# One product of 128 columns for the index key, the gates and the index weights, instead of two

## The reference, cut to what matters

```python
h = rms_norm(x, norm_mix[l])
(m_qk, m_v, m_o, m_i, m_f, r_x, r_g, a_q, a_k, a_v, a_qi, a_ki, a_w, gates) = jnp.split(
    h @ w_in[l], split_at, axis=-1)
...
qi = apply_rope(a_qi.reshape(B, S, IDX_HEADS, IDX_DIM), cos, sin)
ki = apply_rope(a_ki[:, :, None, :], cos, sin)[:, :, 0, :]
...
# in the attention, per block of queries:
logits = jnp.einsum('bqhd,bsd->bqhs', qib.astype(f32), k_idx_f) * (IDX_DIM ** -0.5)
score = jnp.einsum('bqh,bqhs->bqs', wb.astype(f32) * (IDX_HEADS ** -0.5), jax.nn.relu(logits))
```

## Time and profile before

| | us |
|---|---|
| runs, median of 3 (lowest, highest) | 3902.78 (3896.48, 3905.8) |
| profiled execution, device time | 3901.3 |
| profiled execution, span of the core | 3899.5 |
| PE busy | 3705.6 (95%) |
| DVE busy | 2175.3 (56%) |
| ACT busy | 1370.8 (35%) |
| mean granted TensorE clock | 0.972 |

### The profile page before, as it was taken

One profiled execution on the slowest core, in us unless ns is written; L12 is line 12 of the kernel. 1 busy time (PEld: TensorE's weight loads), 2 busy tenths in 40 slices (PEclk: granted clock), 3 DMA queues, 4 the chain that ended last, 5 costly groups with the idle time before them and its releaser, 6 DMA issues. The chain is left out here.

```text
span 3899.5 us, 57931 instructions
## 1 busy us (share of the span) xinstructions
PE 3705.6 (95%) x24033; PEld 3058.4 (78%) x24033; DVE 2175.3 (56%) x2934; ACT 1370.8 (35%) x1537; POOL 0.2 (0%) x4
## 2 busy tenths in 40 slices
PE   7998889999999988899999999899999999899998
PEld 6787778888877877788888777887888778888887
DVE  6896345766358963457663656554232566553233
ACT  5553332443255533324422333033222342033223
POOL 0000000000000000000000000000000000000000
PEclk9999999999999999999999999999999999999999
DMA  3321122554222211225542231022222331032332
GB/s 109 88 73 55 54 68 95 178 199 151 87 82 85 69 55 55 69 94 178 199 149 88 88 126 49 3 105 81 97 97 89 96 119 35 14 118 77 97 97 75
DMA packets 272985, 364.68 MB, mean 94 GB/s; under 512 B 22428, under 2 KB 218640, under 8 KB 271504
## 3 DMA queue, kind: packets, MB, share of 16 engines
q1 hardware_dynamic: 247824, 311.45, 25.0%
q10 hardware_dynamic: 24960, 50.33, 3.7%
HBM read 351.79 MB, written 9.96 MB: 93 GB/s over the span
## 5 line engine op out<-in xcount | busy, mean ns | idle before, releaser
L248 PE MATMUL banks<-act_hi,w_hi 128*128 128x512 f32 x4208 | 1686.7, 401 | 31.8 <-issue 9.9
L250 PE MATMUL banks<-act_hi,w_lo 128*128 128x512 f32 x4208 | 1658.2, 394 | 0.0
L249 PE MATMUL banks<-act_lo,w_hi 128*128 128x512 f32 x4208 | 1657.5, 394 | 0.0
L170 DVE TENSOR_TENSOR w_lo<-w_raw,w_hi 128x2048 fp32r<-128x2048 f32 (+1 forms) x280 | 629.5, 2249 | 746.6 <-ACT w_hi L164 744.9
L248 PEld LDWEIGHTS banks<-act_hi,w_hi 128*128 128x128 f32 x4208 | 803.3, 191 | 238.7 <-issue 59.1
L250 PEld LDWEIGHTS banks<-act_hi,w_lo 128*128 128x128 f32 x4208 | 800.7, 190 | 173.0
L249 PEld LDWEIGHTS banks<-act_lo,w_hi 128*128 128x128 f32 x4208 | 802.7, 191 | 167.2 <-issue 4.3
L164 ACT ACTIVATE w_hi<-w_raw 128x2048 fp32r<-128x2048 f32 (+1 forms) x280 | 526.8, 1882 | 933.7 <-PE banks L250 892.3
L2057 DVE SCALAR_TENSOR_TENSOR arena<-arena,small 128x512 f32<-128x512 f32 (+1 forms) x168 | 126.3, 752 | 15.6 <-issue 4.3
L248 PE MATMUL banks<-w_hi,act_hi 128*128 128x256 f32 x384 | 111.7, 291 | 3.2 <-DVE w_lo L170 3.2
L249 PE MATMUL banks<-w_lo,act_hi 128*128 128x256 f32 x384 | 110.0, 286 | 0.0
(11 more groups left out here) (363 smaller groups left out, 3602.3 us busy)
## 6 DMA issues: line engine op xcount, KB each, us to landing
w_raw<-in_w_in SPq DMA_DIRECT2D x98, 1024.0 KB, 5.4
w_raw<-in_ffn_up SPq DMA_DIRECT2D x48, 1024.0 KB, 5.3
arena<-in_ada_w ACTq DMA_DIRECT2D x24, 2048.0 KB, 8.1
w_raw<-in_w_gu SPq DMA_DIRECT2D x44, 1024.0 KB, 5.0
w_raw<-in_ffn_down SPq DMA_DIRECT2D x24, 1024.0 KB, 4.9
w_raw<-in_w_down SPq DMA_DIRECT2D x20, 1024.0 KB, 5.1
w_raw<-in_w_out SPq DMA_DIRECT2D x16, 1024.0 KB, 4.9
w_raw<-in_w_branch SPq DMA_DIRECT2D x12, 1024.0 KB, 5.0
```

The lines of the kernel that those rows point to most:

```text
L170: self.core.nc.vector.tensor_tensor(view(self.lo[:, s]), view(self.raw[:, s]), view(self.hi[:, s]).bitcast(FP32), ALU.subtract)\
L248: nc.tensor.matmul(out, wh, ah, start=first, stop=False)
L249: nc.tensor.matmul(out, wh, al, start=False, stop=False)
L250: return nc.tensor.matmul(out, wl, ah, start=False, stop=last)
```

## The change

Slot 0 of misc now holds 64 key columns once, 4 gate columns, 28 columns from the index weights on (8 are used) and 32 from the other gate on (4 are used): one product of 24 matmuls, all in bank 1. Slot 1 of misc is loaded with 8 columns that nothing uses, and PE signs it off without a product. The key is rotated on 64 partitions (`key_dve`), and a DVE copy puts it on the other 64.

With this the order changes. ACT rounds aqi's slot 1 first and its slot 0 behind the copies from bank 1; DVE does the rest of slot 1, the key, the forget gate, and then the rest of slot 0. PE still takes aqi's tiles in the order 0, 1, 2, 3. The core of the diff (line numbers after `+` are those of the changed kernel):

```diff
@@ -962,15 +962,16 @@
         def misc(i, s):
-            if s == 0:
-                return [(raw[0][:, :, 0:64], win[:, :, C_AKI:C_AKI + 64]),
-                        (raw[0][:, :, 64:128], win[:, :, C_AKI:C_AKI + 64])]
-
-            return [(raw[1][:, :, 0:32], win[:, :, C_MIF:C_MIF + 32]),
-                    (raw[1][:, :, 32:64], win[:, :, C_MIF + 4:C_MIF + 36]),
-                    (raw[1][:, :, 64:128], win[:, :, C_AW:C_AW + 64])]
+            if s:
+                return [(raw[1][:, :, 0:8], win[:, :, C_MIF:C_MIF + 8])]
+
+            return [(raw[0][:, :, 0:64], win[:, :, C_AKI:C_AKI + 64]),
+                    (raw[0][:, :, 64:68], win[:, :, C_MIF:C_MIF + 4]),
+                    (raw[0][:, :, 68:96], win[:, :, C_AW:C_AW + 28]),
+                    (raw[0][:, :, 96:128], win[:, :, C_MIF + 4:C_MIF + 36])]
 
         part = lambda b: b.rearrange("p (k n) -> p k n", k=8)[:, :, 0:128]
+        unused = lambda b: b.rearrange("p (k n) -> p k n", k=8)[:, :, 0:8]
...
-            Section("misc", 1, misc, view=(part, part), dmas=(2, 3)),
+            Section("misc", 1, misc, view=(part, unused), dmas=(4, 1)),
...
-        aw_rows = A[64:72, self.RX + 3, :]
+        aw_rows = A[64:76, self.RX + 3, :]
...
         def misc_pe(pe):
             um = u["misc"]
+            pe.wait_ge(ring.split[1], um + 1)
+            pe.sem_inc(ring.tile[1], 1)
+            pe.sem_inc(ring.done[1], 1)
             pe.wait_ge(ring.split[0], um + 1)
-            pe.wait_ge(ring.split[1], um + 1)
-            for s in (0, 1):
-                if um:
-                    pe.wait_ge(ring.bank_free[2 * s + 1], um)
-                for k in range(KD):
-                    if s == 0:
-                        pe.wait_ge(n.lo, k + 1)
-                    wh, wl = (b[:, s].rearrange("p (k n) -> p k n", k=8)[:, k, 0:128] for b in (ring.hi, ring.lo))
-                    last = three_pass(nc, ps[:, 2 * s + 1, :], (wh, wl), (self.hi[:, k, :], self.lo[:, k, :]),
-                                      k == 0, k == KD - 1)
-                last.then_inc(ring.done[s], 1)
+            if um:
+                pe.wait_ge(ring.bank_free[1], um)
+            for k in range(KD):
+                pe.wait_ge(n.lo, k + 1)
+                wh, wl = (b[:, 0].rearrange("p (k n) -> p k n", k=8)[:, k, 0:128] for b in (ring.hi, ring.lo))
+                last = three_pass(nc, ps[:, 1, :], (wh, wl), (self.hi[:, k, :], self.lo[:, k, :]), k == 0, k == KD - 1)
+            last.then_inc(ring.done[0], 1)
             pe.sem_inc(ring.tile[0], 1)
-            pe.sem_inc(ring.tile[1], 1)
...
@@ -1345,18 +1344,17 @@
         def act_part(act):
             um = u["misc"]
-            self.schedule.hi(act, um + 1, 0)
-            self.wait_tile(act, um, 1)
-            for q in range(4):
+            self.schedule.hi(act, um + 1, 1)
+            act.wait_ge(ring.done[0], um + 1)
+            for q in (0, 1):
                 ins = nc.scalar.activation(turned[1][32 * q:32 * q + 32, :],
                                            ps[32 * swapped(q):32 * swapped(q) + 32, 1, :], ACT.Copy)
             ins.then_inc(turn_ok, 1)
-            act.wait_ge(ring.done[1], um + 1)
-            nc.scalar.activation(R0, ps[32:36, 3, :], ACT.Copy)
-            nc.scalar.activation(R1, ps[0:4, 3, :], ACT.Copy)
-            nc.scalar.activation(aw_rows, ps[64:72, 3, :], ACT.Copy)
+            nc.scalar.activation(R0, ps[96:100, 1, :], ACT.Copy)
+            nc.scalar.activation(R1, ps[64:68, 1, :], ACT.Copy)
+            nc.scalar.activation(aw_rows, ps[64:76, 1, :], ACT.Copy)
             act.drain().then_inc(rows_ok, 1)
-            self.schedule.hi(act, um + 1, 1)
+            self.schedule.hi(act, um + 1, 0)
...
+        def key_dve(dve):
+
+            low = slice(0, 64)
+            key = A[:, self.KI, :]
+            dve.wait_ge(turn_ok, 1)
+            tt_(key[low], ps[low, 1, :], cos[low], ALU.mult)
+            tt_(turned[1][low], turned[1][low], sin[low], ALU.mult)
+            dve.drain()
+            tt_(key[low], key[low], turned[1][low], ALU.add)
+            dve.drain()
+            nc.vector.tensor_copy(key[64:128], key[low]).then_inc(turn_used, 1)
+
         def forget_dve(dve):
             dve.wait_ge(rows_ok, 1)
+            dve.sem_inc(ring.bank_free[1], 1)
             dve.wait_ge(bias_in, 32)
-            dve.sem_inc(ring.bank_free[3], 1)
...
@@ -1632,12 +1643,12 @@
             if after is None:
                 dve.wait_ge(table_in, 16)
+            for b in (0, 2, 3):
+                dve.sem_inc(ring.bank_free[b], 1)
+            self.schedule.lo(dve, um + 1, 1)
+            key_dve(dve)
+            forget_dve(dve)
             self.schedule.lo(dve, um + 1, 0)
-            rope_dve(dve, 1, A[:, self.KI, :], 1)
-            dve.sem_inc(ring.bank_free[0], 1)
-            dve.sem_inc(ring.bank_free[2], 1)
-            forget_dve(dve)
-            self.schedule.lo(dve, um + 1, 1)
             lambda_dve(dve)
```

More of the change, by code:

```diff
@@ L1141, in aw_pe @@
             for tt in range(ST):
-                last = nc.tensor.transpose(ps[:, 6, 8 * tt:8 * tt + 8], aw_rows[:, tt * P:tt * P + P],
-                                           self.c("ident")[64:72, 64:72])
+                last = nc.tensor.transpose(ps[:, 6, 16 * tt:16 * tt + 12], aw_rows[:, tt * P:tt * P + P],
+                                           self.c("ident")[64:76, 64:76])
             last.then_inc(aw_t, 1)
@@ L1486, in index_weights_dve @@
             dve.wait_ge(aw_t, 1)
-            ts_(gate_tm[:, :, 8:16], ps[:, 6, 0:32].rearrange("p (t c) -> p t c", t=ST), A_HEADS ** -0.5, None, ALU.mult)
+            ts_(gate_tm[:, :, 8:16], ps[:, 6, 0:64].rearrange("p (t c) -> p t c", t=ST)[:, :, 4:12], A_HEADS ** -0.5, None,
+                ALU.mult)
             dve.drain()
```

## The result

Slower, as forecast, and by about what was forecast. In nine runs of each kernel the changed kernel took 3910.18 us in the median (3907.27 to 3912.35) and the kernel before 3896.88 (3896.0 to 3905.8): ratio 1.003, 95% interval [1.002, 1.004], which is 8 to 16 us. The medians lie 13.3 us apart. The forecast was +10.4 us on top of the three runs' 3902.8, rounded to 3912, and slower with a chance of 0.66. The profiled execution took 3912.35 us, its span 3910.6, which is 11.1 more than that of before.

A forecast was written before the change was run, and what follows sets the result against it. PE, busy 95%, and what it waits for were taken to bound the kernel. Two later starts of aqi (3.64 each) and slow clocks (2.0 each), less 0.85, gave +10.4 us on 3902.8: 3912, range 3904 to 3920.

The forecast's parts named there:

- The product was cover: Under the removed misc product, 5.46 us a layer, ACT and DVE did the slot 0 work that aqi needs to start.
- The start of aqi: PE's time between the starts around aqi goes from 6.19 to 9.83 us, +3.64 a layer, waiting for DVE's slot 0 rest.
- the stretch from the rest of slot 1 to the key: On DVE ahead of aqi: 2.42 us from the start of slot 1's rest to the start of the key.
- The copy: DVE's key copy across partitions ahead of aqi: 0.45 us with its gap, bounds 0.42 and 0.69.
- The clock: PE's slow clock in aqi's first tile, behind the 9.8 us idle stretch, costs 2.0 us a layer, bounds 1.3 to 2.6.
- The lower bound: Slow clock's low bound: 2.66 us at granted clock 0.50 behind a 5.24 us wait, times 0.47, 1.3 us a layer.
- The norm: Norm ahead of misc in layer two: narrower slot 1 rounding brings the root earlier, -0.85 us; nothing in layer one.
- Given back: Behind aqi's first tile: DVE idles 2.25 us there, so neither backlog nor credit is carried on, counted as nothing.
- The second rival: Early DVE work removes PE's later waits for DVE's rest, 2.3 us in two places: +5.8 us, 3908; chance 0.07.
- Sum: Whole kernel: 2 x 3.64 + 2 x 2.0 - 0.85 = +10.4 us, forecast 3912 us.

The follow-up runs named there:

- e3_slot0_first: The changed kernel with slot 0 rounded ahead of all copies on ACT and its rest ahead of the key on DVE: 3900.68 us against 3901.78 before.
- e1_slots: The changed kernel with misc's two slots exchanged, so the one product reads slot 1: 3894.04 us against 3901.78 for the kernel before.
- e4_filler: The changed kernel with 40 unread matmuls behind the product of misc in each layer: 3908.64 us, ratio 1.0019 to the kernel before.
- before_again: The kernel before, unchanged, run once more for a second profile: 3903.14 us against 3901.3 in the first.
- e5_early_round: e1_slots with misc's wide slot rounded ahead of the norm's last square in layer two: 3894.3 us against 3901.73 for the kernel before.
- e2_forget_last: The changed kernel with DVE's rest of slot 0 moved ahead of the forget gate's four operations: 3909.89 us, ratio 1.0026 to the kernel before.

## Why the prediction was right

**The product was cover.** As forecast, its removal left the chain rounding, rest and start bare; e3_slot0_first shows it, since slot 0 comes ahead of the copies and the key there and the start still gains only 1.4 of 5.46 us; e1_slots shows that a free slot makes more of the saving real, 3.6 us.

**The start of aqi.** Forecast +3.64 a layer, measured +3.28 and +3.26. The term that was too large is the stretch from the rest of slot 1 to the key: the prediction took 2.42 us from the earlier trace rows, where DVE was itself waiting for ACT's four copies, which ended at 50.75 + 2.40 = 53.15; with the turned key there in time it is 2.21. The rest is ACT, whose rounding starts 0.54 behind the last activation's start and not 0.66, overlapping its end. The copy was taken at 0.45 and measured 0.45 to the next operation; three operations on 64 partitions take what they took on 128. DVE and not ACT came last, by 1.8 us (forecast 2.0).

**The clock.** Forecast 2.0 a layer, measured 1.7 and 2.9 with e4_filler as the comparison. Layer two lies above the bounds from the rows, 1.3 to 2.6. The lower bound was read loosely: of the 9 matmuls in those 2.66 us of the earlier trace rows four were transposes of 128 columns and five had 512, not "about 6". The Trainium skill (TensorE: Matmul & The Clock Gate, Part 1) says that the number of slow matmuls of one kernel varies, 6, 11 or 14 (it doesn't give their width; the prediction took 512 columns), and the prediction's estimate from it reached up to 2.9. The traces agree on the spread, with 9 and 14 behind waits of the same 9.3 us, but here it lay between the layers: the second execution had 9 and 14 again.

**The norm.** Forecast -0.85, measured 1.19 - 0.34 = 0.85. In layer one nothing, as forecast: DVE's wait for PE's transposed parameters grew from 3.23 to 4.22 us instead. The last activation does start 0.8 us earlier there than in the first trace of before (45.54, 46.34), but so it does in before_again (45.36), so this isn't the change's.

**Given back.** Forecast nothing, and in sum it was nothing: PE's later waits for DVE's rest are 0.4 us shorter in layer one and 0.35 longer in layer two. The second rival named this place and took 2.3 us a layer there.

**Sum.** Forecast +10.4, the traces' sum is 4.66 + 6.47 - 0.85 = +10.3. That the terms' errors cancel (0.7 too much at the start, 0.6 too little for the clock) is luck. So is it that 3912 came so near to 3910: it was counted from 3902.8, the median of three runs of before, and with nine runs that median is 3896.88 and the step 13.3.

## What to carry to other kernels

Before a product is taken out, ask what ran under it: on an engine that is 95% busy its length is not the gain, but only what the next chain leaves of it: here 1.4 of 5.5 us with slot 0 first, 3.6 with the slots exchanged, and less than nothing in the order of the change. In a ring of slots, sign off first the slot that the next consumer reads first, and put the long-lived product into the other. A VectorE operation on 4 rows took as long as one on 128 here (0.47 and 0.42 us over 512 elements), so look where it stands: four of them in front of what PE waited for cost 1.8 us.

## What the runs showed of the hardware

- The same wait of 9.3 us was followed by 9 slow matmuls in one layer and 14 in the other, and by the same two numbers in a second execution. Of the four waits of 2.43 to 2.45 us in e1_slots and e5_early_round three were followed by none, and one by slow matmuls from the sixth on.
- A longer wait did not bring more of them: 12 followed the wait of 4.64 us in layer one of e3_slot0_first (8 in layer two, from the third matmul on), and 14 and 10 the waits of 7.54 us in e2_forget_last.
- 40 matmuls in the wait of 9.3 us kept the granted clock at 1.00 behind it (e4_filler).
- A stage of 300 us in which nothing was changed ran at a mean granted clock of 0.94 or 0.92 in two executions of the same kernel.
- A VectorE copy of 512 elements from partitions 0 to 63 to partitions 64 to 127 took 0.42 us, as much as the copy of all 128 partitions onto themselves in the earlier trace rows.
